# An outliving buffer for the expanding weight, the identity, the first queries and the causal corner, and packed sample rows, in a hybrid encoder step

## What is computed

```python
def layer(x, pos, past, ...):
    h = rms_norm(x, attn_norm)
    q_lat, kv_lat, kr_raw, qb_raw, kb_raw, vb_raw, iq_raw, ik_raw, iw = jnp.split(h @ w_in, splits, axis=-1)
    qa = (rms_norm(q_lat, q_a_norm) @ w_q_b).reshape(b, l, 8, 64 + 32)
    qa_nope, qa_rope = qa[..., :64], rope(qa[..., 64:], pos)
    c_kv, k_rope = rms_norm(kv_lat, kv_a_norm), rope(kr_raw, pos)
    qB, kB, vB, iq, ik = ...            # partial rotary on queries and keys of group B and of the indexer
    c_all, kr_all, kB_all, vB_all, ik_all = new, or past and new concatenated (the sample)
    kv = (c_all @ w_kv_b).reshape(b, s_len, 8, 64 + 64)
    o_a = mla_attention(qa_nope, qa_rope, kv[..., :64], kr_all, kv[..., 64:], pos, k_pos)
    o_b = indexed_sparse_attention(qB, kB_all, vB_all, iq, iw, ik_all, pos, k_pos)
    x = x + jnp.concatenate([o_a.reshape(b, l, -1), o_b.reshape(b, l, -1)], axis=-1) @ w_o
    h2 = rms_norm(x, ffn_norm)
    return x + (jax.nn.silu(h2 @ w_gate) * (h2 @ w_up)) @ w_down, new
# a query sees the keys whose chunk of 64 is not later than its own;
# group B: relu(iq . ik) weighted by iw scores the keys, the best min(256, keys // 4) are attended to
# y = rms_norm(layer output, final_norm); the new latents, rotary keys, keys, values and index keys are returned too
```

## Time and profile before

| what | value |
|---|---|
| median of three runs | 3879.97 us |
| lowest and highest | 3871.93 and 3881.75 us |
| the profiled execution, its own time | 3866.08 us |
| its span in the profile | 3864.3 us |
| its mean granted clock of TensorE | 0.968 of full speed |
| TensorE busy (matmuls; weight loads) | 94%; 78% of the span |
| VectorE, ScalarE, GpSimd busy | 54%, 42%, 36% |

### The profile page before, as it was taken

The page is one execution under the profiler, slowest core; times in us unless marked ns, Lnnn a source line. Parts: engine busy times, 40 slices in busy tenths (PEclk is TensorE's granted clock), DMA queues, the critical chain, the costliest instruction groups (busy, mean ns, idle before and its releaser), DMA issues. The chain is left out here.

```text
span 3864.3 us, 54377 instructions
## 1 busy us (share of the span) xinstructions
PE 3636.6 (94%) x19655; PEld 3003.8 (78%) x19655; DVE 2099.4 (54%) x3914; ACT 1610.3 (42%) x2534; POOL 1387.4 (36%) x964
## 2 busy tenths in 40 slices
PE   7999977879989999999998989999999999999998
PEld 6777755667777777888887878887888788789985
DVE  4323335889998898999864544431442244124411
ACT  4333333556666666666654222322332233123311
POOL 0000011656565566555000104444444443443332
PEclk9999987799999999999999999999999999999999
DMA  4232342111000000000003743343334333533321
GB/s 173 86 102 82 95 103 55 47 34 33 25 22 22 22 22 9 20 16 15 9 11 124 282 182 98 98 158 114 98 88 157 120 92 98 161 115 87 87 98 62
DMA packets 323604, 320.74 MB, mean 83 GB/s; under 512 B 37568, under 2 KB 262672, under 8 KB 323360
## 3 DMA queue, kind: packets, MB, share of 16 engines
q1 hardware_dynamic: 308528, 265.79, 23.3%
q0 software_dynamic: 7552, 25.87, 1.9%
q10 hardware_dynamic: 7344, 26.74, 1.7%
HBM read 246.19 MB, written 70.32 MB: 82 GB/s over the span
## 5 line engine op out<-in xcount | busy, mean ns | idle before, releaser
L2047 DVE TENSOR_SCALAR_CACHE_REDUCE at_hit<-at_score,at_su 128x384 bf16<-128x384 f32 (+13 forms) x378 | 558.3, 1477 | 5.1
L1500 DVE TENSOR_TENSOR ff_a_lo<-ff_prod,ff_a_hi 128x512 f32 (+1 forms) x110 | 412.0, 3745 | 170.7 <-ACT ff_a_hi L1452 170.7
L1355 POOL TENSOR_TENSOR fh_w_lo<-fh_stage,fh_w_hi 128x2048 fp32r<-128x2048 f32 x67 | 309.8, 4624 | 463.1 <-ACT fh_w_hi L1438 463.1
L1355 POOL TENSOR_TENSOR ff_w_lo<-fh_stage,ff_w_hi 128x2048 fp32r<-128x2048 f32 (+1 forms) x68 | 296.8, 4365 | 429.2 <-ACT ff_w_hi L1438 412.1
L1865 ACT ACTIVATE at_probt<-at_p_t 128x512 f32<-128x512 f32 (+3 forms) x640 | 312.8, 531 | 228.4 <-PE at_p_t L1788 225.6
L1961 POOL TENSOR_TENSOR at_rel<-at_rel,at_iws 128x512 f32<-128x512 f32 (+3 forms) x304 | 283.8, 933 | 303.4 <-ACT at_rel L1872 214.9
L1788 PE MATMUL at_p_t<-at_ident,at_prob 128*128 128x128 f32 x2176 | 320.0, 283 | 56.3 <-ACT at_prob L1851 54.9
L1851 ACT ACTIVATE at_prob<-at_prob,at_st 128x1024 f32<-128x1024 f32 (+7 forms) x384 | 331.2, 897 | 86.4 <-DVE at_st L2020 85.4
L1803 PEld LDWEIGHTS at_p_o<-kv_VA,at_probt 128*128 128x128 f32 x2176 | 280.1, 200 | 84.9 <-ACT at_probt L1865 47.4
L1788 PEld LDWEIGHTS at_p_t<-at_ident,at_prob 128*128 128x128 f32 x2176 | 258.5, 149 | 89.4 <-ACT at_prob L1851 73.1
L1448 ACT ACTIVATE ff_prod<-ff_bank 128x512 f32<-128x512 f32 (+1 forms) x110 | 57.0, 518 | 646.4 <-PE ff_bank L97 646.2
(11 more groups left out here) (312 smaller groups left out, 7803.3 us busy)
## 6 DMA issues: line engine op xcount, KB each, us to landing
fh_stage<-in_w_gate SPq DMA_DIRECT2D x86, 512.0 KB, 3.9
fh_stage<-in_w_up SPq DMA_DIRECT2D x86, 512.0 KB, 5.1
fh_stage<-in_w_down SPq DMA_DIRECT2D x40, 1024.0 KB, 5.0
pj_xt<-in_xT SPq DMA_DIRECT2D x17, 512.0 KB, 3.7
pj_x<-in_x SPq DMA_DIRECT2D x17, 512.0 KB, 5.0
scr_qT<-pj_qt SPq DMA_DIRECT2D x68, 128.0 KB, 2.3
mx_x<-in_x SPq DMA_DIRECT2D x17, 512.0 KB, 4.0
scr_x<-mx_stage ACTq DMA_DIRECT2D x17, 512.0 KB, 6.3
```

Of the source, the lines that this page charges most:

```text
L1355: pool.tensor_tensor(w_lo[a][:, 0:w], stage[a][:, 0:w], w_hi[a][:, 0:w].bitcast(F32), ALU.subtract).then_inc(s_wlo, 1)
L1500: dve.tensor_tensor(a_lo[:, ds(2 * q + a, 1), to], prod[b][:, 0:gr.Nh].unsqueeze(1), a_hi[:, ds(2 * q + a, 1), to].bitcast(F32), ALU.subtr ...
L2047: step(dve.tensor_scalar(h_, s_, cand.bitcast(F32), 0.0, ALU.is_ge, ALU.add, cnt))
```

## The change

A context that spans project, keys_and_sample and attend_prompt now owns three buffers: pre["w"] (128 x 2048), pre["ident"] and, from the key stage on, pre["corner"].

- In project the identity goes into pre["ident"], and one of the four stage buffers is a part of pre["w"]. Once all low parts of w_in are made, POOL loads w_kv_b into pre["w"] with four DMAs.
- In the key stage the loads of the identity and of w_kv_b and the waits for them go. The loads of kv["VB"] move on SP behind the fourth copy of the rotary key, ahead of load_raw(6). Sample pieces 0, 1 and 2 move from ahead of uses 0, 3 and 5 to ahead of uses 3, 4 and 6. Behind load_raw(7) SP loads the dense queries of tile 0 over the expanding weight's first half and the causal corner into pre["corner"]; POOL writes the columns of ones at the end of its program.
- In the attention the loads of identity, corner and first queries and the waits for them and for the ones go; POOL copies the corner from pre["corner"]. The buffers qa and rel lie in pre["w"].
- In the last group of the feed-forward part the sample's low part is written beside its high part, by an additional subtraction on DVE, into 32 more columns of a_hi. A block's product with the sample is two matmuls: 64 stationary columns (high and low) by the high weights into 64 PSUM rows, and 32 stationary columns (high) by the low weights into the first 32 rows. DVE adds the second 32 rows to the residual first, and then the first 32.

```diff
 project
+            pool.wait_ge(s_wlo, KD)
+            for part in range(2):
+                for k in range(2):
+                    src = io["w_kv_b"][k * P:(k + 1) * P, :].rearrange("p (h a d) -> p h a d", a=2, d=NOPE)[:, :, part, :]
+                    to = pre["w"][:, (2 * part + k) * 512:(2 * part + k + 1) * 512]
+                    pool.dma_start(to.rearrange("p (h d) -> p h d", d=NOPE), src).then_inc(s_pre, 16)
+            pool.wait_ge(s_pre, 64)
...
 keys_and_sample
-        before = {0: [0], 3: [1], 5: [2], 8: [3], 11: [4], 15: [5], 18: [6], 22: [7], 26: [8], 30: [9], 34: [10], 37: [11],
+        before = {3: [0], 4: [1], 6: [2], 8: [3], 11: [4], 15: [5], 18: [6], 22: [7], 26: [8], 30: [9], 34: [10], 37: [11],
...
-            sp.dma_start(ident[:, :], io["ident"]).then_inc(s_const, 16)
             load_raw(0)
-            for part, (sem, to) in enumerate(((s_wk, wk_rows.rearrange("p (k n) -> p k n", k=2)), (s_wv, w_v.rearrange("p k h d -> p k (h d)")))):
-                for k in range(2):
-                    src = io["w_kv_b"][k * P:(k + 1) * P, :].rearrange("p (h a d) -> p h a d", a=2, d=NOPE)[:, :, part, :]
-                    sp.dma_start(to[:, k, :].rearrange("p (h d) -> p h d", d=NOPE), src).then_inc(sem, 16)
             load_raw(1)
-            for g in range(NKV):
-                sp.dma_start(kv["VB"][:, :, g, 0:DH], scr["kbv"][0:SEQ, P + g * DH:P + (g + 1) * DH].rearrange("(j p) d -> p j d", p=P)).then_inc(s_vb, 16)
             for g in range(4):
                 load_raw(g + 2)
                 spread_rope(g)
+            for g in range(NKV):
+                sp.dma_start(kv["VB"][:, :, g, 0:DH], scr["kbv"][0:SEQ, P + g * DH:P + (g + 1) * DH].rearrange("(j p) d -> p j d", p=P)).then_inc(s_vb, 16)
             for v in range(6, 8):
                 load_raw(v)
+            sp.wait_ge(s_wlo, 1)
+            sp.dma_start(pre["w"][0:QK, 0:D].rearrange("p (h t) -> p h t", h=HA), scr["qT"][0, 2, 0:QK, :, :, :].rearrange("p e h t -> p (e h) t")).then_inc(s_qa0, 16)
+            sp.dma_start(pre["corner"][:, :], io["causal_bias"][:, SEQ:SEQ + P]).then_inc(s_corner, 16)
             sp.wait_ge(s_blank, 1)
...
+            pool.memset(kv["VA"][:, :, :, VA:VA + 1], 1.0).then_inc(s_ones, 1)
+            pool.memset(kv["VB"][:, :, :, DH:DH + 1], 1.0).then_inc(s_ones, 1)
...
-            pe.wait_ge(s_const, 16)
...
-            act.wait_ge(s_wk, 32)
             act.activation(wk_hi[:, :, :], wk_rows[:, :], ACT.Copy).then_inc(s_whi, 1)
-            act.wait_ge(s_wv, 32)
             act.activation(wv_hi[:, :, :], w_v[:, :, :, :], ACT.Copy).then_inc(s_whi, 1)
...
 attend_prompt
-            load_qa(0)
-            sp.dma_start(ident[:, :], io["ident"]).then_inc(s_const, 16)
-            sp.dma_start(prob[1][:, 0:P], io["causal_bias"][:, SEQ:SEQ + P]).then_inc(s_const, 16)
             load_qb(0)
             load_qi(2)
...
-            pe.wait_ge(s_const, 32)
-            pe.wait_ge(s_ones, 2)
             product(0, 0, 0)
...
-            pool.memset(kv["VA"][:, :, :, VA:VA + 1], 1.0).then_inc(s_ones, 1)
-            pool.memset(kv["VB"][:, :, :, DH:DH + 1], 1.0).then_inc(s_ones, 1)
+            pool.tensor_copy(tail[:, TAIL - P:TAIL], pre["corner"][:, :]).then_inc(s_zero, 1)
             pool.memset(tail[:, 0:TAIL - P], 0.0).then_inc(s_zero, 1)
-            pool.wait_ge(s_const, 32)
-            pool.tensor_copy(tail[:, TAIL - P:TAIL], prob[1][:, 0:P]).then_inc(s_zero, 1)
...
-            dve.wait_ge(s_const, 32)
...
 ffn
-        a_hi, a_lo = m.sb("a_hi", [P, FB, NMAX], F32R), m.sb("a_lo", [P, FB, NMAX], F32R)
+        a_hi, a_lo = m.sb("a_hi", [P, FB, NMAX + NEW], F32R), m.sb("a_lo", [P, FB, 512], F32R)
...
+                        if gr.halves == 2:
+                            pe.wait_ge(s_als, f0 + fs)
...
-                            mm = split_products(pe, bank[gr.down[n][i]][0:gr.rows(i), :], (a_hi[:, f, tok], a_lo[:, f, tok]),
-                                                (w_hi[a][:, at], w_lo[a][:, at]), f == 0, f == FB - 1)
+                            if gr.tiles[i] == LAST:
+                                to = bank[gr.down[n][i]]
+                                if f == FB - 1:
+                                    pe.matmul(to[0:NEW, :], a_hi[:, f, 512:NMAX], w_lo[a][:, at], start=False, stop=False)
+                                mm = pe.matmul(to[0:2 * NEW, :], a_hi[:, f, 512:NMAX + NEW], w_hi[a][:, at], start=f == 0, stop=f == FB - 1)
+                                if f < FB - 1:
+                                    mm = pe.matmul(to[0:NEW, :], a_hi[:, f, 512:NMAX], w_lo[a][:, at], start=False, stop=False)
+                            else:
+                                mm = split_products(pe, bank[gr.down[n][i]][0:gr.rows(i), :], (a_hi[:, f, tok], a_lo[:, f, tok]),
+                                                    (w_hi[a][:, at], w_lo[a][:, at]), f == 0, f == FB - 1)
...
-                    dve.tensor_tensor(a_lo[:, ds(2 * q + a, 1), to], prod[b][:, 0:gr.Nh].unsqueeze(1),
-                                      a_hi[:, ds(2 * q + a, 1), to].bitcast(F32), ALU.subtract).then_inc(s_alo, 1)
+                    w = min(to.stop, 512) - to.start
+                    if w < gr.Nh:
+                        dve.tensor_tensor(a_hi[:, ds(2 * q + a, 1), NMAX:NMAX + NEW], prod[b][:, w:gr.Nh].unsqueeze(1),
+                                          a_hi[:, ds(2 * q + a, 1), 512:NMAX].bitcast(F32), ALU.subtract).then_inc(s_als, 1)
+                    dve.tensor_tensor(a_lo[:, ds(2 * q + a, 1), to.start:to.start + w], prod[b][:, 0:w].unsqueeze(1),
+                                      a_hi[:, ds(2 * q + a, 1), to.start:to.start + w].bitcast(F32), ALU.subtract).then_inc(s_alo, 1)
...
+                        if gr.tiles[i] == LAST:
+                            dve.tensor_tensor(to, bank[gr.down[n][i]][NEW:2 * NEW, :], to, ALU.add).then_inc(s_ypart, 1)
+                            dve.wait_ge(s_ypart, n + 1)
                         dve.tensor_tensor(to, bank[gr.down[n][i]][0:r, :], to, ALU.add).then_inc(s_y, 1)
```

More of the change, by code:

```diff
@@ L1645, in attend_prompt @@
         prob = [m.sb(f"prob{a}", [P, SEQ]) for a in range(2)]
-        rel = [m.sb(f"rel{a}", [P, 512]) for a in range(2)]
+        rel = [pre["w"][:, D + a * 512:D + (a + 1) * 512] for a in range(2)]
         probt = [m.sb(f"probt{a}", [P, 4, P]) for a in range(2)]
         sums = [m.sb(f"sums{a}", [P, 4, VA + 1]) for a in range(2)]
-        ident = m.sb("ident", [P, P])
+        ident = pre["ident"]
         st = m.sb("st", [P, 72])
```

44 lines of the change are left out of this document (25 added, 19 removed).

## The result

The changed kernel takes 3849.93 us in the median of four runs (3844.25 to 3850.82); the kernel before took 3880.86 us in the median of its four (3871.93 to 3884.42). The ratio is 0.9928 with a 95% interval from 0.9911 to 0.9945, so the change is worth 28 us, at least 21 and at most 35. The profiled execution of the changed kernel took 3850.22 us (span 3848.4 us). That is only 15.9 us less than the profiled execution of before, and the first thing to explain: one of the two profiles is not typical, as the first experiment shows.

A forecast was written before the change was run, and what follows sets the result against it. TensorE (PE), busy for 94% of the span, was taken as the bound. Packing 9.4, key stage 3.3 and attention head 1.9 sum to 14.6 us off the median 3879.97, giving 3865.4 us; range 3856 to 3876.

The forecast's parts named there:

- The base of the sum: Whole kernel: the 14.6 us are taken off the runs' median, 3879.97 us, which was 13.9 us above the profiled execution.
- Packing, 9.4 us: Last feed-forward group: three sample matmuls per block and half become two; 41 of 44 saved ones count, 0.230 us each.
- the tail: End of the last feed-forward group: DVE's second add costs 0, with 0.8 us of cover; without the cover 0.75 us.
- Rival D: Last feed-forward group: packing saves nothing because the 64-column load isn't hidden; 5.2 us gained in all, 3874.8 us, chance 0.06.
- DVE's added subtractions, 0: Last feed-forward group: 22 subtractions of 0.2 us, after POOL's, hidden by DVE's 3.78 us idle; 16 us if caught by POOL.
- Key stage, 3.3 us: Key stage head: raw transposes run before piece 0, so the first K products come sooner; 0.7 at worst, 4.5 at best.
- The move of the VB loads: Key stage, SP: VB loads behind the fourth rope copy, ahead of raw 6, cost 0 with 11.5 us of cover.
- the shift should last to the stage's end: Key stage: later pieces, search and PE-DVE waits move along, so the head's 3.3 us gain should be kept throughout.
- rival B: Stage borders give little, as the clock or next DMA replaces the removed wait; 11.4 us gained, 3868.6 us, chance 0.20.
- Rival E: Key stage: PE's start is cut in two and the clock stays at 1.2 GHz; 23.8 us slower, 3903.8 us, chance 0.04.
- Attention, head, 1.9 us: Attention's start: the corner wait goes, ACT's wait for the index queries is late next; 1.30 at least, 4.3 at best.
- The preload, cost 0: Projection: four weight loads of 256 KB on POOL's queue start at 38.1 us, needed some 480 us later; cost 0.

The follow-up runs named there:

- the first experiment: The kernel before, unedited, run and profiled once more: ratio 1.0003 (0.9993 to 1.0013), second profile 3876.91 us against the first profile's 3866.08.

## Why the prediction was wrong

The forecast missed by one term that it didn't have, the pace of matmuls that the change doesn't touch (8.3 us), and one that it had too small, the key stage (3.3 forecast, 6.7 measured).

- **The base of the sum.** Taking 14.6 us off the median and not off the profiled execution was right: the profile was 11 us below the median of 29 runs, by the clock in tiles 5 to 8 of the attention. Taken off the profile, the forecast would have been 3851.5, close to the result for the wrong reason.
- **Packing, 9.4 us.** Right. The last group is 10.5 us shorter (17.4 less 2.3 for each of groups 0 to 2, whose down products take 121.04 us instead of 123.35). Of these, 616 remaining matmuls x (0.2300 - 0.2277) = 1.4 us are pace, which leaves 9.1. POOL is late at the border by 0.33 us (some 0.4 forecast), and the tail costs nothing with 0.83 us of cover (0.8 forecast). Rival D is out.
- **DVE's added subtractions, 0.** Right in the cost, wrong in the place: the second half-block's subtraction is the one beside POOL, not the one after it. The rows show it:

```profile
3498.36 4.61 POOL L1362 TENSOR_TENSOR ff_w_lo<-fh_stage,ff_w_hi 128x2048 fp32r<-128x2048 f32 x1 [7.43 <-ACT ff_w_hi L1455]
...
3498.78 4.24 DVE L1519 TENSOR_TENSOR ff_a_hi<-ff_prod,ff_a_hi 128x32 f32 x1 [1.82 <-ACT ff_a_hi L1469]
...
3502.94 0.40 DVE L1521 TENSOR_TENSOR ff_a_lo<-ff_prod,ff_a_hi 128x240 f32 x1
...
3508.55 0.44 DVE L1515 TENSOR_TENSOR ff_prod<-ff_bank,ff_prod 128x272 f32<-128x272 f32 x1 [3.69 <-ACT ff_prod L1465]
```

  The 32 columns take 4.24 us because they meet POOL, in the place of the 272 columns that took 4.51, and the other 240 follow in 0.40. DVE's idle time shrinks from 3.78 to 3.69 us. Being caught was priced at 16 us without its cover; it took the place of a cost that was already there.
- **The step that failed: the two buffers had no price.** The prediction's part on the packing lists the matmuls, the border, the tail and DVE's subtractions, and nothing for groups 0 to 2. The diff's line of a_hi and a_lo changes their row distance, and the prediction read it as room for 32 columns. The pace of 0.230 us was taken from the trace as PE's own, and it is the buffer's. Worth 6.9 us in groups 0 to 2 and 1.4 in the last, 8.3 us, and no rival had it.
- **Key stage, 3.3 us.** From first issue to first issue of the attention, the stage takes 126.9, 126.9, 127.2, 130.2 and 132.9 us in five profiles with the old head and 120.2, 120.2, 120.4, 120.5, 124.5 and 127.5 in six with the new one, 6.7 us between the medians. Three things were mis-sized. The index keys land 1.5 us sooner (6.7 instead of 8.2 us behind the first issue), half as much again as the "1 us sooner" of the upper bound, and piece 0 takes 0.88 us instead of 1.28; so the search begins 5.2 us sooner. The move of the VB loads stood at "cost 0" with 11.5 us of cover on SP: the cover is right (SP issues them from 595.01 to 599.41 and raw 6 not before 615.03), but the move is needed for the gain. In the kernel before, SP issued them only from 525.83, 0.3 us ahead of the index keys' landing; with the weight's loads gone, their old place has them issued from 520.11, in the way of POOL's. And "the shift should last to the stage's end" failed in the stage's favour, by 1.5 us, through the clock. In the kernel before it falls in this stretch:

```profile
549.90:553.90 4.00, 4.00 (x28) 3.54 (x28) 1.56 (x8) 0.95 (x2) 0.00 (x0) 0.76 0.00 0
553.90:557.90 4.00, 2.98 (x16) 2.59 (x15) 1.38 (x2) 2.05 (x4) 0.00 (x0) 0.82 0.18 22
```

  In four of the six profiles with the new head it stays at 1.00 from 8 to 76 us behind the first issue, and the stage takes 120.2 to 120.5 us; in the other two it falls to 0.50 near 28 us, and the stage takes 124.5 and 127.5. No experiment was made on this fall, so the 5.2 us by the search are shown as the change's own, and what the stage as a whole keeps of them hangs on the clock too.
- **The clock at the head.** In the change's table of stretches:

```profile
523.00:525.00 2.00, 1.98 (x10) 1.96 (x11) 0.20 (x1) 0.60 (x1) 2.00 (x5) 0.50 0.93 312
525.00:526.60 1.60, 1.60 (x9) 0.99 (x7) 1.18 (x2) 1.19 (x2) 1.60 (x3) 0.67 0.03 1
526.60:528.00 1.40, 1.40 (x7) 1.05 (x7) 0.00 (x0) 0.62 (x1) 1.40 (x4) 1.00 0.73 93
```

  PE had made nothing but transposes when the clock rose, ahead of the first K product at 526.64, so the choice by the earlier trace rows was right, and rival B with it is out. The Trainium skill ("TensorE: Matmul & The Clock Gate", Part 4) has transposes not count; this trace disagrees. Transposes don't always bring the clock back, though: with the pieces in their old places PE makes transposes alone from 550.98 to 555.09, and the clock is still at 0.50 over 554.50 to 558.50.
- **Rival E** is not what happened, but its mechanism is real: the early VB loads cut PE's start in two, and PE ran at 1.2 GHz for some 6 us behind the gap, and not through all four K blocks.
- **Attention, head, 1.9 us.** Right, 1.6 at ACT's rounding, with ACT late next as said. Whether all of it reaches the stage's end can't be told beside the clock's play.
- **The preload, cost 0.** Nearly: PE's last matmul of the projection starts at 514.6 us in the mean of seven profiles with the preload (the run with the projection's rows changed left out) and at 513.6 in six without. What that microsecond is was not tried.

The sum of the traces is 17.4 + 6.7 + 1.6 - 1.0 = 24.7 us, within the measured 21 to 35; the last few us aren't told apart from the clock's play in the attention.

## What to carry to other kernels

Read a changed buffer shape as a change of every instruction that uses the buffer: here 32 more columns in one row were worth almost as much as the packing that they were for, and the same edit on the next buffer shortened the feed-forward part by 16 us more for one line. Before a wait is priced by the load that it names, ask which other loads lie in the DMA queues with it, and whether PE, once started, will stop again: a gap of 2.2 us went with 5.2 us lost. And take a second profile of the kernel before, when one execution lies below all its timed runs.
